# The second mixer's attention: every second head's turned probabilities are copied by ScalarE, and a head's score bank is released by VectorE's first read

## The chip, the cores and the metric

One core of a Trainium2 chip runs the whole kernel. The metric is the device time of one execution in microseconds (us); of several runs the median is taken. TensorE multiplies matrices and writes its results to PSUM, eight banks called bank[0] to bank[7]; VectorE (DVE) and ScalarE (ACT) read them there; GpSimd (POOL) fills a few tiles; SyncE (SP) starts the transfers.

## What is computed

Three transformer layers on 256 tokens of width 1024, all in 32-bit floats. The second layer's mixer is the one of the change. It projects the tokens (`proj = h @ w_in`), cuts the result and runs two attentions of 8 heads of width 64 each:

```python
def mixer_cd(h, w_in, w_out, rel_table):
    ...
    o_c = moba_attention(qc.reshape(B, S, H, dh), kc.reshape(B, S, G, dh), vc.reshape(B, S, G, dh),
                         rel_table[:, :H])
    o_d = stick_breaking_attention(qd.reshape(B, S, H, dh), kd.reshape(B, S, H, dh), vd.reshape(B, S, H, dh))
    return jnp.concatenate([o_c, o_d], axis=-1) @ w_out
```

With 256 tokens the first (moba) is a causal softmax attention with a bias by distance: softmax(scale * q k + bias) v. The second (stick-breaking) has no softmax. With z = scale * q k and a strict causal mask, its weight is

```python
        log_1m = jnp.where(strict, jax.nn.log_sigmoid(-z), 0.0)
        after = lax.cumsum(log_1m, axis=3, reverse=True) - log_1m
        w = jnp.where(strict, jnp.exp(jax.nn.log_sigmoid(z) + after), 0.0)
        o = jnp.einsum('bhqk,bkhd->bqhd', w.astype(dt), v)
```

## The kernel before, in words

Each engine has its own program, written out in order, and they meet only at semaphores: `then_inc(name, 1)` on an instruction counts up when it ends, `wait_ge(name, n)` holds an engine's queue until the count is n. Nothing is scheduled by a planner; the order of the lines is the order on each engine. The weights stream in as units of 128x1024, each split into a high part (ScalarE, L836) and a low part (VectorE, L1403), and each product is done as three matmuls (L2131 to L2133).

The stage of the change lies between the projections of the second mixer (18 units) and its output projection (`cd_out`, 8 units). It is a loop over rounds s = 0 to 9 on TensorE, 0 to 8 on VectorE and ScalarE. One round handles one moba head and one stick-breaking head side by side; scores tiles are 128x384 (the first 128 queries against 128 keys, the second 128 against 256). Moba heads are numbered 24 to 31 in the semaphores.

TensorE in round s, in this order:
- `scores_and_z(s)`, L2690 to L2694: the scores of both heads, moba into bank[4], stick-breaking (z) into bank[5]. It waits until VectorE has read both banks of the round before (neg_ready, and zabs_ready, which L1876 counts).
- `transposes` (L2301) of moba head s-1, 3 of 128x128 into bank[6]. It waits for the probabilities and for `pt_ready`: the copy of the head before out of the same bank[6].
- `stick_suffix(s-1)`, L2703 to L2705: the sums over later keys, into bank[7]. It waits for L1912.
- `pv` (L2311 to L2313): turned probabilities of head s-2 times its values. It waits for their copy (`pt_ready`).
- in odd rounds from 3, `stick_out`, L2715 and L2718: weights times values for a pair of stick-breaking heads. Then the next round's scores. In round 8 the first unit of the output projection (L2131 to L2133) stands behind `pv`, and round 9 has `pv` of the last head.

VectorE in round s:
- `neg_scores` (L1550, L1552): bias added to the moba scores, and the row's minimum; two instructions, each with a small one that reads out the minimum.
- `stick_in(s)`: L1873 adds the mask to z (the first read of bank[5], and the only one), L1876 takes the absolute value from the SBUF copy.
- L1904: suffix sums added to z of head s-1, for the weight.
- `take_pt` (L1560): copies the turned probabilities of moba head s-1 from bank[6] to pt, 128x384. It waits for the transposes and for the `pv` of the head before (pv_done), since both use the same tile pt[:, 0].
- L1912, for head s, after ScalarE's logarithm; then the next round.

ScalarE in round s:
- `exp_rows` (L963): the exponentials of the moba head in two pieces, each with a read-out of its row sum.
- `stick_log`: L1195 (exponential) and L1196 (logarithm).
- L1216: the exponential that gives the weights of stick-breaking head s-1.
- near the end `stick_high` (L971) and the splits (L836) of the output projection's units.

The earlier mixer has a copy of turned probabilities on ScalarE (`ab_take_pt`, L1117); in this stage all 8 are VectorE's L1560.

Of the kernel before, what the change touches and what calls it, by code (L numbers as in the profile page):

```python
# [24 lines left out]
ALU = mybir.AluOpType  # L25
# [15 lines left out]
EPS = 1e-6  # L41
BIG = 1e30
# [139 lines left out]
def build_program(nc, A):  # L182
    with ExitStack() as ctx:
# [85 lines left out]
        rel_landed = sem("rel_landed")  # L269
        cs_ready = sem("cs_ready")  # L270
        raw_full = [sem(f"raw_full{i}") for i in range(RING)]
# [8 lines left out]
        shift_psum = sem("shift_psum")  # L280
        kc_zero = sem("kc_zero")
        cw_landed = sem("cw_landed")
# [13 lines left out]
        sh_ready = sem("sh_ready")  # L296
        warm_ready = sem("warm_ready")
        crow_psum = sem("crow_psum")
# [36 lines left out]
        oTH_ready = sem("oTH_ready")  # L335
        z_psum = sem("z_psum")
        zabs_ready = sem("zabs_ready")
        zlog_ready = sem("zlog_ready")
# [15 lines left out]
        csil_ready = sem("csil_ready")  # L354
        eps_ready = sem("eps_ready")
        dve_done = sem("dve_done")
# [434 lines left out]
        @block.gpsimd  # L791
        def _(pool):
            nc.gpsimd.memset(warm, 1.0).then_inc(warm_ready, 1)
            nc.gpsimd.memset(kc[:, :, :], 0.0).then_inc(kc_zero, 1)
            nc.gpsimd.memset(epst[:, :], EPS).then_inc(eps_ready, 1)

            pool.wait_ge(rstd_ready, 1)
            nc.gpsimd.memset(cs, BIG).then_inc(cs_ready, 1)

            pool.wait_ge(table_out, 16)  # L800
            pool.wait_ge(mod_used, 11)
            pool.wait_ge(shift_psum, 1)
            for half in range(2):
                if half == 1:
                    pool.wait_ge(misc_taken, misc["cscore"] + 1)
                for a in (0, 4, 1, 5, 2, 6, 3, 7):

                    diag = bass.AP(A["table"].tensor, 4 * half * 1024 + 2 * (P - 1 - a),
                                   [[8 * 1024 - 2 * 8, COPIES], [1024, 4], [1, 2 * S]])
                    pool.dma_start(strips[a:P:8, 4 * half:4 * half + 4].rearrange("p a s j -> p a (s j)"),  # L810
                                   diag).then_inc(strips_landed[half], 16)

        @block.scalar
        def _(act):
# [255 lines left out]
            nc.scalar.preload_act_table_set("natural_log_exp_and_others")  # L1070
            act.wait_ge(eps_ready, 1)
            norm_a(0)
# [133 lines left out]
            for h in range(H + 1):  # L1206
                if 1 <= h < H:
                    act.wait_ge(pt_psum, 24 + h)
                    exp_rows(24 + h, 0)
                if 1 <= h < H:  # L1210
                    stick_log(h)
                if h == H:
                    stick_high(2)
                if h >= 1:
                    act.wait_ge(fw_ready, h)
                    nc.scalar.activation(stick_w[(h - 1) % 3], stick_w[(h - 1) % 3], ACT.Exp).then_inc(w_ready, 1)  # L1216
                if h == H - 1:
                    stick_high(0, 2)
# [166 lines left out]
        def _(dve):  # L1385
# [410 lines left out]
            for s in range(AB_STEPS):  # L1796
# [20 lines left out]
                if s == 2:  # L1817
                    take("vrep")
                    rep = bank[7][:, 0:P].rearrange("p (g d) -> p g d", g=G)
                    for t in range(4):  # L1820
                        hm = bcast(const("headmask").rearrange("p (g t) -> p t g", g=G)[:, t].unsqueeze(2), [P, G, HD])
                        V.tensor_tensor(vcb(t).rearrange("p (g d) -> p g d", g=G), rep, hm, ALU.mult)
                    dve.wait_ge(kc_zero, 1)
                    link(V.tensor_copy(kc[0:HD, 0, 0:NCMP], bank[7][0:HD, P:P + NCMP]))
                    taken(V.tensor_copy(kc[HD:P, 1, 0:NCMP], bank[7][HD:P, P:P + NCMP]))
                if s == 3:
                    take("cscore")
                    dve.wait_ge(cs_ready, 1)
                    for q in range(QT):
# [38 lines left out]
            def stick_in(h):  # L1868

                dve.wait_ge(z_psum, h + 1)  # L1870
                if h >= 2:
                    dve.wait_ge(fw_ready, h - 1)
                link(V.tensor_tensor(stick_z_buf[h % 2], bank[5][:, 0:384], mask, ALU.add))  # L1873
                if h >= 2:
                    dve.wait_ge(suf_psum, h - 1)
                V.scalar_tensor_tensor(out=stick_sp[h % 2], in0=stick_z_buf[h % 2], scalar=-1.0,  # L1876
                                       in1=stick_z_buf[h % 2], op0=ALU.mult, op1=ALU.max).then_inc(zabs_ready, 1)
# [14 lines left out]
            for s in range(H + 1):  # L1892
# [3 lines left out]
                if s >= 1:  # L1896
# [5 lines left out]
                    if h >= 3:  # L1902
                        dve.wait_ge(stick_pv, h - 2)
                    V.tensor_tensor(stick_w[h % 3], bank[7][:, 0:384], stick_z_buf[h % 2],  # L1904
                                    ALU.add).then_inc(fw_ready, 1)
                    take_pt(24 + h)
                if s == 1:
# [214 lines left out]
        def _(pe):  # L2122
# [315 lines left out]

            pe.wait_ge(warm_ready, 1)
            def keep_warm(bk, n):  # L2440
# [240 lines left out]
            def scores_and_z(s):  # L2681
# [6 lines left out]
                pe.wait_ge(neg_ready, 24 + s)  # L2688
                pe.wait_ge(zabs_ready, s)
                mm(bank[4][:, P:3 * P], mq[:, P:2 * P], mk, start=True, stop=True, skip_group_check=True)  # L2690
# [311 lines left out]
```

## Time and profile before

| | us |
|---|---|
| median of 3 runs (942.99 to 943.42) | 943.39 |
| the profiled execution, its own time | 944.02 |
| its span, first to last instruction | 942.2 |
| busy: TensorE | 919.1 |
| busy: TensorE's weight loads | 837.8 |
| busy: VectorE | 796.2 |
| busy: ScalarE | 564.9 |
| busy: GpSimd | 8.9 |

All numbers of the trace are from the one profiled execution; its own time is 1.8 us above its span and 0.6 us above the median of the runs. The granted clock of TensorE is the share of its full clock that it was allowed; its mean is 0.999. Matmuls overlap, so the distance from start to start tells more than their durations. A timeline row gives the start in us from the span's start, the duration in us, the engine, the line, the operation, what it writes and reads, how many instructions the row merges (x2), and in brackets the idle time of the engine before it with what ended it.

### The profile page before, as it was taken

To read this page: it belongs to the slowest core of one execution; us is meant where nothing else is said; L and a number is where in the kernel's file an instruction comes from. 1 tells how busy PE (TensorE), PEld (TensorE's weight loads), DVE (VectorE), ACT (ScalarE), POOL (GpSimd) and SP (SyncE) were. 2 spreads that over 40 slices of the span, in tenths; PEclk is the share of its full clock that TensorE was granted. 3 is DMA by queue.
4 is the path that set the end of the run, shared out by engine and by line. 5 is a ranking of instruction groups with operands and counts; after the bars stand their busy time and mean duration, and the time that the engine had idled before them with its cause. 6 is when DMAs were issued, how large, how long until landed. Compare 5 with 4: busy or idle time off the path is not lost. (4 is left out here: it accounts for less than half of the span.)

```text
span 942.2 us, 17752 instructions
## 1 busy us (share of the span) xinstructions
PE 919.1 (98%) x6693; PEld 837.8 (89%) x6693; DVE 796.2 (85%) x1441; ACT 564.9 (60%) x1173; POOL 8.9 (1%) x24
## 2 busy tenths in 40 slices
PE   8999999999999999999999999999999999999997
PEld 5787768999999989977999999998989999999995
DVE  5879897998888879898899988878889778887775
ACT  3447776555444576574745454447857677767774
POOL 0101000000000000000000000000000000000000
PEclk9999999999999999999999999999999999999999
DMA  9996774899988739904499988872832545555531
GB/s 353 397 360 227 263 255 182 317 349 322 342 313 312 257 111 342 345 30 155 166 325 355 315 305 310 312 253 94 333 113 79 200 165 199 190 195 180 180 111 46
DMA packets 63223, 227.46 MB, mean 241 GB/s; under 512 B 7187, under 2 KB 7827, under 8 KB 63158
## 3 DMA queue, kind: packets, MB, share of 16 engines
q1 hardware_dynamic: 62102, 223.86, 66.6%
q0 software_dynamic: 768, 2.10, 0.8%
q8 instruction: 39, 0.64, 0.3%
q10 hardware_dynamic: 288, 0.66, 0.2%
q14 instruction: 26, 0.21, 0.1%
HBM read 225.01 MB, written 1.57 MB: 240 GB/s over the span
## 5 line engine op out<-in xcount | busy, mean ns | idle before, releaser
L2131 PE MATMUL bank<-hH,wH 128*128 128x258 f32 (+1 forms) x1344 | 382.8, 285 | 0.0
L2132 PE MATMUL bank<-hL,wH 128*128 128x258 f32 (+1 forms) x1344 | 379.7, 283 | 0.0
L2133 PE MATMUL bank<-hH,wL 128*128 128x258 f32 (+1 forms) x1344 | 379.2, 282 | 0.0
L1403 DVE TENSOR_TENSOR wL<-raw,wH 128x1024 fp32r<-128x1024 f32 x264 | 320.4, 1219 | 12.7 <-ACT wH L836 10.4
L836 ACT ACTIVATE wH<-raw 128x1024 fp32r<-128x1024 f32 x264 | 269.8, 1047 | 17.3 <-PE bank L2133 14.6
L2131 PEld LDWEIGHTS bank<-hH,wH 128*128 128x128 f32 x1344 | 253.2, 188 | 6.1 <-issue 3.3
L2132 PEld LDWEIGHTS bank<-hL,wH 128*128 128x128 f32 x1344 | 254.6, 189 | 2.3
L2133 PEld LDWEIGHTS bank<-hH,wL 128*128 128x128 f32 x1344 | 254.8, 190 | 0.0
L2131 PE MATMUL bank<-wH,aH 128*128 128x512 f32 x280 | 110.1, 393 | 0.0
L2133 PE MATMUL bank<-wH,aL 128*128 128x512 f32 x280 | 109.1, 390 | 0.0
L2132 PE MATMUL bank<-wL,aH 128*128 128x512 f32 x280 | 109.0, 389 | 0.0
L988 ACT ACTIVATE fcol<-bank 128x1 f32<-128x1 f32 x132 | 14.9, 164 | 112.0 <-PE bank L2133 111.9
L1427 DVE CUSTOM_DVE_ANT_0 modbuf<-modbuf,crow,gw 128x1024 f32<-128x1024 f32 x48 | 62.9, 1317 | 0.0
L2133 PEld LDWEIGHTS bank<-wH,aL 128*128 128x128 f32 x280 | 52.5, 188 | 11.0
L2131 PEld LDWEIGHTS bank<-wH,aH 128*128 128x128 f32 x280 | 52.5, 187 | 10.7 <-issue 2.5
L2132 PEld LDWEIGHTS bank<-wL,aH 128*128 128x128 f32 x280 | 52.6, 188 | 8.3
L1427 DVE CUSTOM_DVE_ANT_0 modbuf<-modbuf,crow,sc 128x1024 f32<-128x1024 f32 x41 | 54.8, 1337 | 0.4 <-DMA modbuf<-in_mods 0.3
L1040 ACT ACTIVATE aH<-sn 128x256 fp32r<-128x256 f32 x66 | 27.6, 418 | 42.8 <-DVE sn L1663 21.5
L1427 DVE CUSTOM_DVE_ANT_0 modbuf<-modbuf,crow,mv 128x1024 f32<-128x1024 f32 x40 | 51.1, 1277 | 1.8 <-DMA modbuf<-in_mods 1.8
L1622 DVE TENSOR_TENSOR sn<-bank,rstd 128x256 f32<-128x256 f32 x44 | 18.6, 422 | 35.9 <-ACT fcol L988 35.9
L1005 ACT ACTIVATE sn<-sn,fcol 128x256 f32<-128x256 f32 x44 | 22.5, 511 | 42.2 <-DVE sn L1622 42.2
L1648 DVE SCALAR_TENSOR_TENSOR pr<-sq,par,pr 128x255 f32<-128x255 f32 x44 | 19.3, 481 | 26.5 <-ACT pr L1020 26.5
(377 smaller groups left out, 1222.0 us busy)
## 6 DMA issues: line engine op xcount, KB each, us to landing
raw<-in_weights SPq DMA_DIRECT2D x264, 512.0 KB, 4.8
modbuf<-in_mods SPq DMA_DIRECT2D x129, 512.0 KB, 6.7
raw<-in_mods SPq DMA_DIRECT2D x10, 512.0 KB, 10.9
strips<-bias_table POOLq DMA_DIRECT2D x16, 128.0 KB, 6.0
strips<-in_mods SPq DMA_DIRECT2D x3, 512.0 KB, 15.0
modbuf<-in_weights SPq DMA_DIRECT2D x3, 512.0 KB, 14.1
x<-in_xT SPq DMA_DIRECT2D x2, 512.0 KB, 4.2
proj<-in_mods SPq DMA_DIRECT2D x2, 512.0 KB, 14.7
```

Source lines behind the costliest of these rows:

```text
L836: nc.scalar.activation(wH[:, slot, :], raw[:, slot, :], ACT.Copy).then_inc(hi_ready[c], 1)
L988: last = nc.scalar.activation(fcol[:, t % 2, n:n + 1], bk[:, S:S + 1], ACT.Copy)
L1005: nc.scalar.activation(sn[:, t % 2, 0:S], sn[:, t % 2, 0:S], ACT.Silu, bias=fcol[:, t % 2, 0:1]).then_inc(silu_ready, 1)
L1040: nc.scalar.activation(aH[:, a_slot(phase, t), :], sn[:, t % 2, S:2 * S], ACT.Copy).then_inc(aH_ready, 1)
L1403: V.tensor_tensor(wL[:, slot, :], raw[:, slot, :], wH[:, slot, :].bitcast(F32), ALU.subtract).then_inc(lo_ready[c], 1)
L1427: V.tensor_tensor_reduce(src, src, crow[:, m // 4, :], weight, total, ALU.mult, ALU.add, total).then_inc(mod_used, 1)
L1622: V.tensor_tensor(sn[:, t % 2, 0:S], gate_bank[:, 0:S], rstd[:, :], ALU.mult).then_inc(g_scaled, 1)
L1648: chain.inc(V.scalar_tensor_tensor(out=dst[:, 1:S], in0=z[:, 0:S - 1], scalar=row[:, 4 * n:4 * n + 1], in1=dst[:, 1:S], op0=ALU.mult, op1= ...
L2131: mm(out, lhs_h, rhs_h, start=start, stop=False, skip_group_check=True)
L2132: mm(out, lhs_h, rhs_l, start=False, stop=False, skip_group_check=True)
L2133: return mm(out, lhs_l, rhs_h, start=False, stop=stop, skip_group_check=True)
```

## The change

ScalarE gets a copy in rounds 2, 4, 6 and 8, behind L1216: the turned probabilities of moba heads 1, 3, 5 and 7 of the stage. VectorE's `take_pt` stays for heads 0, 2, 4 and 6. VectorE's L1873 counts a new semaphore, z_taken, on which both VectorE itself (in the place of a chain semaphore) and TensorE's `scores_and_z` wait; TensorE waited for zabs_ready (L1876) before. Four semaphores of GpSimd's fills at the start become one, pool_set, with counts 1 to 4. The diff:

```diff
--- before.py
+++ after.py
@@ -267,7 +267,6 @@
         con_landed = sem("con_landed")
         x_landed = [sem(f"x_landed{i}") for i in range(2)]
         rel_landed = sem("rel_landed")
-        cs_ready = sem("cs_ready")
         raw_full = [sem(f"raw_full{i}") for i in range(RING)]
         hi_ready = [sem(f"hi_ready{i}") for i in range(3)]
         lo_ready = [sem(f"lo_ready{i}") for i in range(3)]
@@ -278,7 +277,6 @@
         mod_used = sem("mod_used")
         c_landed = sem("c_landed")
         shift_psum = sem("shift_psum")
-        kc_zero = sem("kc_zero")
         cw_landed = sem("cw_landed")
         cwv_landed = sem("cwv_landed")
         table_half = sem("table_half")
@@ -294,7 +292,7 @@
         x_ready = sem("x_ready")
         y_ready = sem("y_ready")
         sh_ready = sem("sh_ready")
-        warm_ready = sem("warm_ready")
+        pool_set = sem("pool_set")
         crow_psum = sem("crow_psum")
         crow_ready = sem("crow_ready")
         unit_full = [sem(f"unit_full{i}") for i in range(6)]
@@ -334,6 +332,7 @@
         oT_ready = sem("oT_ready")
         oTH_ready = sem("oTH_ready")
         z_psum = sem("z_psum")
+        z_taken = sem("z_taken")
         zabs_ready = sem("zabs_ready")
         zlog_ready = sem("zlog_ready")
         sp_ready = sem("sp_ready")
@@ -352,7 +351,6 @@
         zc_ready = sem("zc_ready")
         conv_ready = sem("conv_ready")
         csil_ready = sem("csil_ready")
-        eps_ready = sem("eps_ready")
         dve_done = sem("dve_done")
         act_done = sem("act_done")
         qk_sq = sem("qk_sq")
@@ -790,12 +788,12 @@
 
         @block.gpsimd
         def _(pool):
-            nc.gpsimd.memset(warm, 1.0).then_inc(warm_ready, 1)
-            nc.gpsimd.memset(kc[:, :, :], 0.0).then_inc(kc_zero, 1)
-            nc.gpsimd.memset(epst[:, :], EPS).then_inc(eps_ready, 1)
+            nc.gpsimd.memset(warm, 1.0).then_inc(pool_set, 1)
+            nc.gpsimd.memset(kc[:, :, :], 0.0).then_inc(pool_set, 1)
+            nc.gpsimd.memset(epst[:, :], EPS).then_inc(pool_set, 1)
 
             pool.wait_ge(rstd_ready, 1)
-            nc.gpsimd.memset(cs, BIG).then_inc(cs_ready, 1)
+            nc.gpsimd.memset(cs, BIG).then_inc(pool_set, 1)
 
             pool.wait_ge(table_out, 16)
             pool.wait_ge(mod_used, 11)
@@ -1068,7 +1066,7 @@
                     nc.scalar.preload_act_table_set("natural_log_exp_and_others")
 
             nc.scalar.preload_act_table_set("natural_log_exp_and_others")
-            act.wait_ge(eps_ready, 1)
+            act.wait_ge(pool_set, 3)
             norm_a(0)
             act.wait_ge(par_landed, 16)
             first_row(0)
@@ -1214,6 +1212,10 @@
                 if h >= 1:
                     act.wait_ge(fw_ready, h)
                     nc.scalar.activation(stick_w[(h - 1) % 3], stick_w[(h - 1) % 3], ACT.Exp).then_inc(w_ready, 1)
+                if h >= 2 and h % 2 == 0:
+                    act.wait_ge(pt_psum, 24 + h)
+                    act.wait_ge(pv_done, 24 + h - 1)
+                    nc.scalar.activation(pt[:, 0, 0:384], bank[6][:, 0:384], ACT.Copy).then_inc(pt_ready, 1)
                 if h == H - 1:
                     stick_high(0, 2)
             split_upto(base + 24)
@@ -1820,12 +1822,12 @@
                     for t in range(4):
                         hm = bcast(const("headmask").rearrange("p (g t) -> p t g", g=G)[:, t].unsqueeze(2), [P, G, HD])
                         V.tensor_tensor(vcb(t).rearrange("p (g d) -> p g d", g=G), rep, hm, ALU.mult)
-                    dve.wait_ge(kc_zero, 1)
+                    dve.wait_ge(pool_set, 2)
                     link(V.tensor_copy(kc[0:HD, 0, 0:NCMP], bank[7][0:HD, P:P + NCMP]))
                     taken(V.tensor_copy(kc[HD:P, 1, 0:NCMP], bank[7][HD:P, P:P + NCMP]))
                 if s == 3:
                     take("cscore")
-                    dve.wait_ge(cs_ready, 1)
+                    dve.wait_ge(pool_set, 4)
                     for q in range(QT):
                         n = (7, NCMP)[q]
                         dst = cs[:, q * P:(q + 1) * P].rearrange("p (g t n) -> p g t n", g=G, n=16)[:, :, :, 0:n]
@@ -1870,7 +1872,8 @@
                 dve.wait_ge(z_psum, h + 1)
                 if h >= 2:
                     dve.wait_ge(fw_ready, h - 1)
-                link(V.tensor_tensor(stick_z_buf[h % 2], bank[5][:, 0:384], mask, ALU.add))
+                V.tensor_tensor(stick_z_buf[h % 2], bank[5][:, 0:384], mask, ALU.add).then_inc(z_taken, 1)
+                dve.wait_ge(z_taken, h + 1)
                 if h >= 2:
                     dve.wait_ge(suf_psum, h - 1)
                 V.scalar_tensor_tensor(out=stick_sp[h % 2], in0=stick_z_buf[h % 2], scalar=-1.0,
@@ -1903,7 +1906,8 @@
                         dve.wait_ge(stick_pv, h - 2)
                     V.tensor_tensor(stick_w[h % 3], bank[7][:, 0:384], stick_z_buf[h % 2],
                                     ALU.add).then_inc(fw_ready, 1)
-                    take_pt(24 + h)
+                    if h % 2 == 0:
+                        take_pt(24 + h)
                 if s == 1:
                     values(VALUES["cd"][17])
                 if s < H:
@@ -2436,7 +2440,7 @@
                             mm(out[:, c], row, start_values[:, c, cols], start=False, stop=True,
                                skip_group_check=True).then_inc(unit_used[c], 1)
 
-            pe.wait_ge(warm_ready, 1)
+            pe.wait_ge(pool_set, 1)
             def keep_warm(bk, n):
 
                 for _ in range(n):
@@ -2686,7 +2690,7 @@
                 mq, mk = proj[m_rows, h % 4, :], proj[m_rows, 4, :]
                 zq, zk = proj[z_rows, 5 + s // 2, :], proj[z_rows, 9 + s // 2, :]
                 pe.wait_ge(neg_ready, 24 + s)
-                pe.wait_ge(zabs_ready, s)
+                pe.wait_ge(z_taken, s)
                 mm(bank[4][:, P:3 * P], mq[:, P:2 * P], mk, start=True, stop=True, skip_group_check=True)
                 mm(bank[5][:, 0:S], zk[:, 0:P], zq, start=True, stop=True, skip_group_check=True)
                 mm(bank[4][:, 0:P], mq[:, 0:P], mk[:, 0:P], start=True, stop=True,
```

## Rows read from the trace of the kernel before

**Rows 1.** The page's first line.
```profile
span 942.2 us, 17752 instructions
```

**Rows 2.** Busy by stretch: length, PE, PEld, DVE, ACT, POOL, clock, DMA, GB/s.
```profile
404.82:408.23 3.41, 3.15 (x23) 2.63 (x23) 3.07 (x11) 2.54 (x7) 0.00 (x0) 1.00 0.00 0
...
411.81:415.23 3.42, 3.31 (x26) 2.75 (x26) 3.08 (x9) 2.54 (x7) 0.00 (x0) 1.00 0.00 0
415.23:418.81 3.58, 3.44 (x29) 2.85 (x30) 3.15 (x10) 2.54 (x7) 0.00 (x0) 1.00 0.00 0
```

**Rows 3.** Timeline of VectorE, rounds 2 and 3.
```profile
406.90 0.55 DVE L1560 COPY pt<-bank 128x384 f32<-128x384 f32 x1
407.75 0.56 DVE L1912 SCALAR_TENSOR_TENSOR otok<-sq,otok 128x384 f32<-128x384 f32 x1 [0.31 <-ACT otok L1196]
408.23 0.28 DVE L1550 CUSTOM_DVE_ANT_0 sn<-bank,strips 128x128 f32<-128x128 f32 x1
...
409.85 0.55 DVE L1904 TENSOR_TENSOR pt<-bank,sq 128x384 f32<-128x384 f32 x1
410.31 0.55 DVE L1560 COPY pt<-bank 128x384 f32<-128x384 f32 x1
411.16 0.56 DVE L1912 SCALAR_TENSOR_TENSOR otok<-sq,otok 128x384 f32<-128x384 f32 x1 [0.30 <-ACT otok L1196]
411.81 0.29 DVE L1550 CUSTOM_DVE_ANT_0 sn<-bank,strips 128x128 f32<-128x128 f32 x1
```

**Rows 4.** Timeline of ScalarE, the same rounds.
```profile
407.63 0.51 ACT L1216 ACTIVATE sn<-sn 128x384 f32<-128x384 f32 x1
408.96 0.40 ACT L963 ACTIVATE pr<-sn,nm 128x128 f32<-128x128 f32 x1 [0.82 <-DVE nm L1552]
...
410.52 0.62 ACT L1196 ACTIVATE otok<-otok,con 128x384 f32<-128x384 f32 x1
411.04 0.51 ACT L1216 ACTIVATE pt<-pt 128x384 f32<-128x384 f32 x1
```

**Rows 5.** Timeline of TensorE, rounds 2 to 4.
```profile
403.25 0.45 PE L2690 MATMUL bank<-proj 64*128 64x256 f32 x1 [0.66 <-DVE otok L1876]
...
407.59 0.52 PE L2301 MATMUL bank<-con,pr 128*128 128x128 f32 x3
408.37 0.49 PE L2703 MATMUL bank<-otok,con 128*128 128x128 f32 x2 [0.26 <-DVE otok L1912]
...
409.35 0.33 PE L2311 MATMUL bank<-vt,pt 128*128 128x64 f32 x2
...
410.06 0.43 PE L2715 MATMUL bank<-pr,vt 128*64 128x256 f32 x1
...
410.86 0.48 PE L2690 MATMUL bank<-proj 64*128 64x256 f32 x1
...
411.71 0.55 PE L2301 MATMUL bank<-con,pr 128*128 128x128 f32 x3
412.10 0.39 PE L2703 MATMUL bank<-otok,con 128*128 128x128 f32 x2
...
412.97 0.34 PE L2311 MATMUL bank<-vt,pt 128*128 128x64 f32 x2
```

**Rows 6.** The earlier mixer's copy on ScalarE: durations in ns, min/median/max.
```profile
L1117 ACT ACTIVATE pt<-bank x24: 463/476/492, 68.3 to 135.6; 128x384 f32<-128x384 f32 x24
```

**Rows 7.** Timeline of all engines, the stage's end.
```profile
426.76 0.33 PE L2311 MATMUL bank<-vt,pt 128*128 128x64 f32 x2
...
427.55 0.52 ACT L1216 ACTIVATE sn<-sn 128x384 f32<-128x384 f32 x1 [1.25 <-DVE sn L1904]
427.65 0.56 DVE L1560 COPY pt<-bank 128x384 f32<-128x384 f32 x1
427.98 1.04 ACT L836 ACTIVATE wH<-raw 128x1024 fp32r<-128x1024 f32 x1
...
430.23 0.33 PE L2311 MATMUL bank<-vt,pt 128*128 128x64 f32 x2
```

## The prediction

> **What bounds the kernel now.** I read the page first: the span is 942.2 us [rows 1] and TensorE is at work nearly all of it, so anything that makes TensorE wait and is not caught up later is paid in full. Then I cut the stage of the change, the attention of the second mixer, into its rounds. A round of the loop over heads handles one head; its mark is VectorE's bias-and-minimum (L1550). The stretches are cut at these marks: round 2 from 404.82, round 3 from 408.23, round 4 from 411.81, round 5 from 415.23, round 6 from 418.81. An even round takes 3.41 or 3.42 us, an odd one 3.58, so a pair costs 7.00 us; in round 2 TensorE is busy for 3.15 us and the granted clock is 1.00, its upper level of 2.4 GHz [rows 2]. Then I followed one pair on each engine in time order.
>
> VectorE [rows 3]: from mark to mark it has no hole but one, before L1912, 0.31 us in one round and 0.30 us in the next, and it ends on ScalarE's L1196. In the round that starts at 408.23 it also waits before the next mark: L1912 to L1550 is 0.48 us when free (407.75 to 408.23) and 0.65 us there (411.16 to 411.81), the difference of 0.17 us being TensorE's scores.
>
> ScalarE [rows 4]: the exponentials (L963) start 0.73 us after the mark (408.23 to 408.96), the logarithm's second half (L1196) 1.56 us after that, L1216 0.52 us later, and then nothing until the next L963: 0.82 us of idle time in the round from 408.23. L1912 starts 0.64 us after L1196. So the loop is VectorE's mark, ScalarE's exponentials and logarithm, VectorE's L1912, mark: 0.73 + 1.56 + 0.64 + 0.48 = 3.41 us, which is the round. VectorE's copy of the turned probabilities (L1560) is beside this loop, under ScalarE's logarithm.
>
> TensorE [rows 5]: transposes (L2301), suffix sums (L2703), the product with the values (L2311), every second round the product of the stick-breaking heads (L2715), then the next scores (L2690). The transposes of head 2 start at 407.59, which is 0.14 us after the end of VectorE's copy of head 1 (406.90 + 0.55 = 407.45 [rows 3]): they go into the one bank that this copy empties. This hand-over is what the change moves.
>
> **The change part by part.** *The copy of heads 1, 3, 5 and 7 leaves VectorE.* Four times L1560, each some 0.46 us of VectorE's issue (L1904 at 409.85 to L1560 at 410.31 [rows 3]). VectorE then only waits longer for L1196 before L1912: 0.30 us becomes about 0.76 us. Gain on the path: none; the cover is ScalarE's chain from L963 to L1196. If that cover were gone, it would be worth up to 4 x 0.46 = 1.84 us.
>
> *The same copy on ScalarE, behind L1216.* The earlier mixer already has this instruction, 128x384 from a bank on ScalarE: 0.476 us in the median, 0.463 to 0.492 [rows 6]. What follows L1216 starts about 0.43 us after it (427.55 to 427.98 [rows 7]). In ScalarE's own queue it costs nothing: 0.91 us fall into the hole before L963, behind L1216 at 407.63 it would run 408.06 to 408.54, and L963 is due at 408.96. That leaves 0.42 us. The two waits ahead of it (transposes of the head, values product of the head before) are over by then.
>
> The copy is later, though: 408.06 instead of 406.90. Its waiter is TensorE. Taking 0.13 us to TensorE (0.14 from VectorE; I take nearly the same), the transposes of head 2 start at 408.67 instead of 407.59, 1.08 us late. Behind them in the queue stand the suffix sums, the values product, the stick-breaking product and the scores of round 4. From here with the free spacings of [rows 5]: transposes to suffix 0.39 (411.71 to 412.10), suffix to values product 0.87 (412.10 to 412.97), then 0.71 and 0.80, so suffix 409.06, product 409.93, L2715 410.64, scores 411.44 against 410.86. The hold-ups of before (TensorE waited 0.26 us at L2703) absorb half of the 1.08 us. The scores reach VectorE 0.95 us after their start (410.86 to 411.81), so the mark of round 4 comes at 412.39 against 411.81: **+0.58 us**.
>
> The loop of two rounds is now another one, through ScalarE's copy and TensorE's queue: mark to L963 0.73, L1196 1.56, L1216 0.52, copy 0.43, its length 0.48, to TensorE 0.13, suffix 0.39, product 0.87, L2715 0.71, scores 0.80, next even mark 0.95. Sum 7.57 us against 7.00: **+0.57 us**, once, from round 4 to round 6. That makes 1.15 us at the mark of round 6, 419.96.
>
> *The third hand-over* has no scores behind it. From 419.96 the transposes of head 6 start 3.85 us later, at 423.81; suffix 424.20, product 425.07, L2715 425.78, transposes of head 7 426.58, suffix of head 7 not before 426.97. The other gate is VectorE: the mark of round 7 at 419.96 + 3.41 = 423.37, L1912 by ScalarE at 423.37 + 2.93 = 426.30, but the copy that VectorE keeps (head 6) waits for the end of the values product, 0.89 us after that product's start (426.76 to 427.65 [rows 7]), so 425.96, and with 0.46 us L1912 comes at 426.42. In the round of 407.75 L2703 starts 0.62 us after L1912 [rows 3, 5], so suffix 7 starts at 427.04 and, with the 0.98 us that a held suffix takes before the values product (408.37 to 409.35 [rows 5]), that product starts at 428.02 against 426.76 [rows 7]: +1.26 us. Earlier, in rounds 3 and 5, the same small delay of L1912 (0.1 us) is hidden, since VectorE waits for the scores anyway. Sum **+1.2 to 1.3 us**; I take 1.2.
>
> *The fourth* costs nothing: behind suffix 7 TensorE goes to the output projection, and the values product of head 7 stands at 430.23, 2.7 us after L1216 at 427.55 [rows 7], where copy and way need 1.04 us. If that projection were not there it would cost some 0.5 us.
>
> *Head's bank freed by the first read.* TensorE waits for z_taken (L1873) instead of zabs_ready (L1876), some 0.6 us earlier. Only the row at 403.25 shows TensorE idle for it, 0.66 us [rows 5]. Its scores are for the mark at 404.82, which they would meet at 403.25 + 0.95 = 404.20 already, and the transposes behind them wait for VectorE's copy as before. Worth nothing now; at most 0.17 us at each of two marks if the hand-over before them were not late. The wait on VectorE itself replaces a wait of the same kind.
>
> *Semaphores merged for GpSimd's fills.* Same instructions in the same order, each waiter asks for the count of its own fill: nothing, with a bound of 0.1 us either way.
>
> **A page against the rows.** The Trainium skill, "TensorEngine Tiling (Array Packing)", PSUM Bottleneck, advises to use ScalarE as well as VectorE to empty PSUM; it would make this change a gain, and it is my second rival below. "PSUM — Partial Sum Buffer", Engine vs sequencer instructions, calls ScalarE's queue strictly first in, first out; by that the copy cannot slip ahead of L1216 into an earlier place, and the rows of ScalarE agree, being in program order. Without these two sentences the sum stands as it is.
>
> **Forecast.** 1.2 us later than the kernel before. Against the profiled execution, whose span is 942.2 us and whose own time is 944.02 us, that is a span of 943.4 and a time of 945.2 us. Against the median of the runs, 943.39 us (0.6 lower than the profiled one), it is **944.6 us**. About 0.2%, 1.9 us here, is what a measurement of this kernel can tell from no change; the forecast lies inside it, on the slow side. Chance 0.70.
>
> **Rivals.** *Slower, beyond 0.2%: the lateness isn't absorbed.* Place: TensorE's queue behind L2301 in rounds 3, 5 and 7. The price is the whole 1.08 us each time, 3 x 1.08 = 3.2 us, 946.6 us. It decides if TensorE's stretch between the copy and the next even mark grows by as much play as it now has, 0.5 us: L1912 of the odd rounds has only 0.1 us of play against VectorE's remaining copy, and a late L1912 holds the suffix sums. Against it: each free spacing is a row of the trace. A lower granted clock in the longer holes of TensorE would act likewise, but the rows show 1.00 across the present ones. Chance 0.13.
>
> *Faster: VectorE's issue is the bound.* Its row is 3.07 us busy of 3.41 [rows 2]. If L1912 really followed VectorE's own queue, the four copies would give back 1.84 us and the earlier bank 2 x 0.17: 941.2 us. This is what the tiling page would have. Against it: L1912 idles for ScalarE in both rounds. Chance 0.04.
>
> *Nothing: the copy's move is hidden and so is the rest.* It needs TensorE to have 1.08 us of play between L2301 and the even mark; it has about 0.5. Or the delay is made up later, in the projection, where TensorE rarely waits. 943.4 us, at best 0.34 less for the marks' waits: 943.1. Chance 0.13.
>
> **Numbers.** The range leaves out the fast rival and most of the slow one: 943.2 to 946.0. It holds the bounds of the way to TensorE (0.05 to 0.25 us, three times) and of L1912's play. Faster by over 0.2%: 0.03. Within: 0.80, which is the "nothing" case and nearly all of the forecast. Slower: 0.17, the slow rival and the upper edge of the forecast.
>
> **What the next profile would show.** Right: four ScalarE copies of 0.48 us right behind L1216 in the even rounds; L2301 of rounds 3, 5, 7 released by ScalarE with about 1 us of idle TensorE ahead; pairs of rounds at 7.57 us; VectorE idle near 0.76 us before L1912 in even rounds, and before the even marks 0.6 us or more for TensorE; suffix 7 near 427.0. Wrong: even marks on their old places, a copy that starts earlier than L1216, or pairs of 8 us.

## The result, and the profile after

The changed kernel takes 944.85 us in the median of 20 runs (943.65 to 946.13), the kernel before 943.43 us (942.50 to 945.93, 20 runs beside them). The ratio is 1.0013, 95% interval 1.0007 to 1.0019: 1.2 us slower, 0.7 to 1.8 us (the two medians differ by 1.4 us). That is inside the 0.2% that was called no change, and on the slow side, as forecast (944.6 us). The spans of the two profiled executions can't show it alone: 942.7 us against 942.2 [rows 1]. The stage itself can, since there are hardly any transfers in it and its distances repeat from pair to pair.

The lines of the changed kernel are shifted: the mark of a round is L1552 (was L1550), VectorE's copy L1562 (L1560), its others L1879 (L1876), L1907 (L1904) and L1916 (L1912); on ScalarE L961, L1193, L1194, L1214 (L963, L1195, L1196, L1216) and the new copy L1218; on TensorE L2305 (L2301), L2707 (L2703), L2315 (L2311), L2719 (L2715), L2694 and L2696 (L2690 and L2692). The experiments shift them by a few lines more; the operation and its tiles tell which is meant.

Busy time of the changed kernel by stretch, from mark to mark, rounds 2 to 5 (columns as in [rows 2]):

```profile
404.06:407.48 3.42, 2.61 (x20) 2.26 (x20) 2.62 (x10) 2.64 (x8) 0.00 (x0) 1.00 0.00 0
407.48:411.60 4.12, 3.70 (x32) 3.13 (x33) 3.29 (x11) 2.70 (x8) 0.00 (x0) 1.00 0.02 4
411.60:415.02 3.42, 2.79 (x23) 2.44 (x23) 2.62 (x9) 2.63 (x8) 0.00 (x0) 1.00 0.00 0
415.02:419.14 4.12, 3.70 (x32) 3.13 (x33) 3.29 (x10) 2.71 (x8) 0.00 (x0) 1.00 0.00 0
```

Even rounds are as long as before, odd ones 4.12 us instead of 3.58 [rows 2]: a pair costs 7.54 us instead of 7.00. VectorE did lose its work, 2.62 us busy in round 2 instead of 3.07, and got nothing for it. The granted clock stays at 1.00.

ScalarE in rounds 2 and 3 of the changed kernel:

```profile
406.87 0.51 ACT L1214 ACTIVATE sn<-sn 128x384 f32<-128x384 f32 x1
407.29 0.47 ACT L1218 ACTIVATE pt<-bank 128x384 f32<-128x384 f32 x1
408.46 0.40 ACT L961 ACTIVATE pr<-sn,nm 128x128 f32<-128x128 f32 x1 [0.70 <-PE bank L2305]
...
409.35 0.51 ACT L1193 ACTIVATE otok<-otok 128x384 f32<-128x384 f32 x1
```

TensorE:

```profile
401.90 0.45 PE L2694 MATMUL bank<-proj 64*128 64x256 f32 x1
...
403.43 0.52 PE L2305 MATMUL bank<-con,pr 128*128 128x128 f32 x3 [0.60 <-DVE pt L1562]
...
407.90 0.52 PE L2305 MATMUL bank<-con,pr 128*128 128x128 f32 x3 [1.08 <-ACT pt L1218]
408.25 0.39 PE L2707 MATMUL bank<-otok,con 128*128 128x128 f32 x2
...
409.13 0.33 PE L2315 MATMUL bank<-vt,pt 128*128 128x64 f32 x2
...
410.64 0.48 PE L2694 MATMUL bank<-proj 64*128 64x256 f32 x1
```

VectorE, from the end of round 2 to the mark of round 4:

```profile
407.00 0.56 DVE L1916 SCALAR_TENSOR_TENSOR otok<-sq,otok 128x384 f32<-128x384 f32 x1 [0.77 <-ACT otok L1194]
407.48 0.28 DVE L1552 CUSTOM_DVE_ANT_0 sn<-bank,strips 128x128 f32<-128x128 f32 x1
...
410.02 0.56 DVE L1562 COPY pt<-bank 128x384 f32<-128x384 f32 x1
410.54 0.56 DVE L1916 SCALAR_TENSOR_TENSOR otok<-sq,otok 128x384 f32<-128x384 f32 x1
411.60 0.29 DVE L1552 CUSTOM_DVE_ANT_0 sn<-bank,strips 128x128 f32<-128x128 f32 x1 [0.51 <-PE bank L2696]
```

Read in this order, the rows show the path of the delay. The copy runs 407.29 to 407.76. TensorE, idle for 1.08 us, starts the transposes at 407.90, 3.84 us after the mark of round 2 (404.06); before it was 2.77 us (404.82 to 407.59 [rows 3, 5]). Three pieces of TensorE's work later the scores of round 4 start at 410.64, and VectorE, idle for 0.51 us, gets them at 411.60.

For the experiments one measure serves: **the stretch** from TensorE's first scores of the loop to its values product of head 6, the last one ahead of the output projection. Before it is 26.89 us (399.87 to 426.76), after 28.10 us (399.12 to 427.22): +1.21 us. The 0.75 us by which the loop itself starts earlier in the second profile lie ahead of every copy that was moved. The start lies at 398.92 to 399.87 in the fourteen profiles of this study, and at 398.92, 399.13, 399.29, 399.32, 399.37 and 399.87 in the six whose program ahead of the loop is that of the kernel before. What is lost in the stretch isn't made up later: from its end to the end of the span there are 515.4 to 515.6 us in all fourteen.

### The profile page after: what moved, and what is told of

Same layout as the page of the kernel before. It is cut to its first block and busy times, and to the rows that moved or that the text cites. A ratio compares the mean times of both kernels' runs of the same rounds, so it can differ in the third digit from the quotient of the medians.

```text
span 942.7 us, 17752 instructions
## 1 busy us (share of the span) xinstructions
PE 917.7 (97%) x6693; PEld 837.5 (89%) x6693; DVE 794.9 (84%) x1437; ACT 566.2 (60%) x1177; POOL 8.9 (1%) x24
## 5 line engine op out<-in xcount | busy, mean ns | idle before, releaser
L1038 ACT ACTIVATE aH<-sn 128x256 fp32r<-128x256 f32 x66 | 27.6, 417 | 42.6 <-DVE sn L1665 21.5
L1650 DVE SCALAR_TENSOR_TENSOR pr<-sq,par,pr 128x255 f32<-128x255 f32 x44 | 19.3, 481 | 26.8 <-ACT pr L1018 26.8
```

Source lines behind the costliest of these rows:

```text
L1038: nc.scalar.activation(aH[:, a_slot(phase, t), :], sn[:, t % 2, S:2 * S], ACT.Copy).then_inc(aH_ready, 1)
L1650: chain.inc(V.scalar_tensor_tensor(out=dst[:, 1:S], in0=z[:, 0:S - 1], scalar=row[:, 4 * n:4 * n + 1], in1=dst[:, 1:S], op0=ALU.mult, op1= ...
```

## The experiments

Theory A is that of the forecast: what costs is the late hand-over of bank[6] to TensorE, through what stands behind it in TensorE's queue. Theory B: ScalarE's additional copy costs as such. Theory C: the release of bank[5] by z_taken matters. Where the text gives "one time", the kernel ran once; such a time can't tell differences of this size, and the stretch is read there.

### Each half of the change alone

Both start from the changed kernel. The copies alone:

```diff
-                pe.wait_ge(z_taken, s)
+                pe.wait_ge(zabs_ready, s)
```

> The change without its second half: ScalarE copies heads 1, 3, 5 and 7, but TensorE's scores wait for zabs_ready (the second read's count) as before. Measure: TensorE from its first scores of the loop to the values product of head 6 (30 in the semaphores' numbering): 26.89 us in the kernel before, 28.10 in the changed one. Theory A (the late hand-over of bank[6] costs, nothing else): 28.0 to 28.2 us, time 1.2 us over the kernel before. Theory C (the earlier release of bank[5] costs or saves something): the stretch departs from 28.10 by over 0.2 us.

The release alone:

```diff
-                if h >= 2 and h % 2 == 0:
-                    act.wait_ge(pt_psum, 24 + h)
-                    act.wait_ge(pv_done, 24 + h - 1)
-                    nc.scalar.activation(pt[:, 0, 0:384], bank[6][:, 0:384], ACT.Copy).then_inc(pt_ready, 1)
...
-                    if h % 2 == 0:
-                        take_pt(24 + h)
+                    take_pt(24 + h)
```

> The change without its first half: VectorE copies all eight heads, TensorE's scores wait for z_taken, and GpSimd's fills share one semaphore. Theory A: the stretch is 26.8 to 26.95 us as before, the scores of round 2 start 0.6 us earlier and that shortens nothing; time within 0.2 us of the kernel before. Theory C: over 0.3 us away from 26.89.

The copies alone: stretch 28.10 us (399.49 to 427.59), 944.91 us, ratio 1.0013 (1.0004 to 1.0022). The release alone: stretch 26.90 us (399.17 to 426.07), 943.75 us, ratio 1.0002 (0.9993 to 1.0011). In the stretch the first half is the whole effect and the second is nothing, though it does what it says; the times agree, with intervals of 0.8 to 0.9 us either way. TensorE's transposes and scores around round 2, first with the copies alone, then with the release alone:

```profile
402.87 0.45 PE L2694 MATMUL bank<-proj 64*128 64x256 f32 x1 [0.67 <-DVE otok L1879]
...
403.81 0.52 PE L2305 MATMUL bank<-con,pr 128*128 128x128 f32 x3
```

```profile
401.96 0.45 PE L2689 MATMUL bank<-proj 64*128 64x256 f32 x1
...
403.48 0.52 PE L2300 MATMUL bank<-con,pr 128*128 128x128 f32 x3 [0.60 <-DVE pt L1558]
```

With the release alone the wait for the second read (0.67 us) is gone, and 0.60 us of TensorE's idle time stand before the next group instead, the transposes, which wait for VectorE's copy.

### The same copies at another place

The changed kernel, with ScalarE's copy moved up by one instruction (e3):

```diff
                 if 1 <= h < H:
                     stick_log(h)
...
+                if h >= 2 and h % 2 == 0:
+                    act.wait_ge(pt_psum, 24 + h)
+                    act.wait_ge(pv_done, 24 + h - 1)
+                    nc.scalar.activation(pt[:, 0, 0:384], bank[6][:, 0:384], ACT.Copy).then_inc(pt_ready, 1)
                 if h >= 1:
                     act.wait_ge(fw_ready, h)
                     nc.scalar.activation(stick_w[(h - 1) % 3], stick_w[(h - 1) % 3], ACT.Exp).then_inc(w_ready, 1)
-                if h >= 2 and h % 2 == 0:
-                    act.wait_ge(pt_psum, 24 + h)
-                    act.wait_ge(pv_done, 24 + h - 1)
-                    nc.scalar.activation(pt[:, 0, 0:384], bank[6][:, 0:384], ACT.Copy).then_inc(pt_ready, 1)
```

> The changed kernel with ScalarE's copy one instruction earlier, ahead of the exponential of the weights instead of behind it: same work on ScalarE, the copy ends 0.4 to 0.5 us sooner. Theory A: lateness at the transposes of heads 2, 4 and 6 falls from 1.08 to about 0.6 us, of which 0.5 is absorbed; pairs of rounds at 7.05 to 7.15 us instead of 7.54, the stretch at 27.0 to 27.3 us, time 0.1 to 0.4 over the kernel before. Theory B (it is ScalarE's extra work or the copy out of PSUM beside VectorE that costs, wherever it stands): the stretch stays at 28.0 or more.

The changed kernel, with the even heads on ScalarE and the odd ones on VectorE (e4):

```diff
-                if h >= 2 and h % 2 == 0:
+                if h % 2 == 1:
                     act.wait_ge(pt_psum, 24 + h)
-                    act.wait_ge(pv_done, 24 + h - 1)
+                    if h >= 2:
+                        act.wait_ge(pv_done, 24 + h - 1)
...
-                    if h % 2 == 0:
+                    if h % 2 == 1:
                         take_pt(24 + h)
```

> The same number of copies on ScalarE, but of heads 0, 2, 4 and 6, behind the exponential of the weights in the odd rounds; VectorE copies 1, 3, 5 and 7. The late hand-over now stands before the transposes of the even rounds, which have no product of the stick-breaking heads behind them and whose scores come 0.6 us before VectorE wants them. Theory A: the lateness is absorbed, the stretch is 26.9 to 27.3 us, time 0 to 0.4 us over the kernel before. Theory B: as in the changed kernel, 28 us or more.

The copy ahead of the weights' exponential: stretch 27.15 us (399.48 to 426.63), 943.92 us, ratio 1.0003 (0.9994 to 1.0012). The marks of rounds 4 and 6, 7.13 us apart:

```profile
411.55 0.29 DVE L1552 CUSTOM_DVE_ANT_0 sn<-bank,strips 128x128 f32<-128x128 f32 x1 [0.22 <-PE bank L2696]
...
418.68 0.29 DVE L1552 CUSTOM_DVE_ANT_0 sn<-bank,strips 128x128 f32<-128x128 f32 x1 [0.22 <-PE bank L2696]
```

The same four copies, 0.42 us sooner, and 0.95 of the 1.21 us are gone: the work of the copies as such (theory B) isn't what costs. The 0.26 us left lie in rounds 3 and 5, 3.72 and 3.71 us long instead of 3.58, at whose ends VectorE waits for the scores as the rows show.

The even heads: stretch 27.60 us (399.37 to 426.97), 944.45 us, ratio 1.0010 (0.9999 to 1.0020). Within the loop it came as expected: the marks of rounds 4 and 6 lie at 411.48 and 418.48, 7.00 us apart as before, with ScalarE making a copy in each odd round. The 0.71 us, where 0 to 0.4 were expected, come at its two ends: 0.13 in round 2 (3.54 us long), 0.54 in round 8. TensorE's transposes, rounds 2, 4 and 8:

```profile
404.78 0.52 PE L2306 MATMUL bank<-con,pr 128*128 128x128 f32 x3 [1.66 <-ACT pt L1219]
...
411.74 0.52 PE L2306 MATMUL bank<-con,pr 128*128 128x128 f32 x3 [0.29 <-ACT pt L1219]
...
425.73 0.52 PE L2306 MATMUL bank<-con,pr 128*128 128x128 f32 x3 [1.14 <-ACT pt L1219]
```

In round 4 the wait of 0.29 us is absorbed: no stick-breaking product follows, and the next scores have time. In round 8 the transposes start 3.83 us after the mark of round 7 (421.90) instead of 2.78, 1.05 us late. Half of that is taken up on the way to the values product, which starts 5.07 us after that mark instead of 4.53; no mark of VectorE follows that could take up the rest, and behind it comes the projection. I had left out the end of the loop when I wrote down 27.3 us.

### What the lateness runs into

TensorE's scores ahead of the stick-breaking product, on the kernel before (e6) and on the changed one (e7):

```diff
+            scores_and_z(1)
             for s in range(H + 2):
-                if 1 <= s < H:
-                    scores_and_z(s)
                 if 1 <= s <= H:
...
+                if 1 <= s < H - 1:
+                    scores_and_z(s + 1)
                 if s >= 3 and s % 2 == 1:
                     stick_out((s - 3) // 2)
```

> The kernel before with TensorE's scores of the next round ahead of the product of the stick-breaking heads in rounds 3 and 5. Theory A: VectorE no longer waits 0.17 us before the marks of rounds 4 and 6; all rounds 3.41 us, the stretch 26.5 to 26.6 us instead of 26.89. Nothing a time can show.

> The changed kernel with the same move on TensorE: scores of the next round ahead of the product of the stick-breaking heads. Theory A: ScalarE's copy is as late as in the changed kernel and TensorE still waits about 1.0 us for it at the transposes of heads 2, 4 and 6, but the way from there to the even marks is 0.80 us shorter, so that the loop through the copy is 6.77 us and no longer bounds: pairs at 6.9 to 7.0 us, the stretch 26.7 to 27.1 us, time within 0.3 us of the kernel before. Theory B (the wait of TensorE itself is what costs, wherever the scores stand): 28 us.

On the kernel before: all rounds 3.41 us, the stretch 26.58 us (399.13 to 425.71), as expected, with one time of 943.02 us. On the changed kernel: 27.38 us (399.09 to 426.47), 944.09 us, ratio 1.0009 (1.0000 to 1.0018). TensorE still waits for the copy:

```profile
407.92 0.52 PE L2305 MATMUL bank<-con,pr 128*128 128x128 f32 x3 [1.08 <-ACT pt L1218]
...
415.08 0.52 PE L2305 MATMUL bank<-con,pr 128*128 128x128 f32 x3 [0.67 <-ACT pt L1218]
```

The stretch is 0.72 us shorter than in the changed kernel, but 0.31 of that is what this order also gives without the offload (26.89 to 26.58). Like with like, the offload costs 0.80 us in this order (27.38 against 26.58) instead of 1.21: the shorter way to the marks takes away 0.41 us, a third. And 27.38 is over the 27.1 expected. ScalarE in round 4 of this run shows what I had overlooked:

```profile
410.43 0.51 ACT L1214 ACTIVATE pt<-pt 128x384 f32<-128x384 f32 x1
412.10 0.40 ACT L961 ACTIVATE pr<-sn,nm 128x128 f32<-128x128 f32 x1 [1.17 <-PE bank L2305]
```

The mark of round 4 is at 411.03, and the exponentials start 1.07 us after it instead of 0.73: there is one tile for the probabilities of all heads, so they wait until TensorE has turned those of the head before. Late transposes thus hold ScalarE too, and the rounds become 3.54 us (odd) and 3.62 us (even) instead of 3.41. In the changed kernel the same gate is in its rows above (L961 at 408.46, 0.98 us after the mark), without effect there, since round 3 then waits for the scores anyway.

Both repairs together (e9) are the edits of e3 and e7 on the changed kernel.

> The changed kernel with both repairs: ScalarE's copy ahead of the exponential of the weights, and TensorE's scores of the next round ahead of the product of the stick-breaking heads. What e7_change_scores_first left was a second gate: ScalarE's exponentials wait for the transposes of the head before (one tile of probabilities), at 412.10, 0.34 us later than the mark alone would allow. With the copy 0.4 us earlier that gate should be met. Theory A: rounds at 3.41 to 3.46 us, the stretch 26.5 to 26.8 us, that is the kernel before with its waits for the scores removed and no gain from the four copies that VectorE no longer makes. If VectorE's issue did count, it would be under 26.2 us.

Stretch 26.56 us (399.37 to 425.93), one time of 943.20 us. All marks are 3.41 us apart:

```profile
404.33 0.28 DVE L1552 CUSTOM_DVE_ANT_0 sn<-bank,strips 128x128 f32<-128x128 f32 x1
...
407.74 0.28 DVE L1552 CUSTOM_DVE_ANT_0 sn<-bank,strips 128x128 f32<-128x128 f32 x1
...
411.16 0.28 DVE L1552 CUSTOM_DVE_ANT_0 sn<-bank,strips 128x128 f32<-128x128 f32 x1
...
414.57 0.28 DVE L1552 CUSTOM_DVE_ANT_0 sn<-bank,strips 128x128 f32<-128x128 f32 x1
```

With the copies on ScalarE and no harm from their lateness the stretch is what e6 has with all copies on VectorE, 26.56 against 26.58 us. That is the value of VectorE's four saved copies in this order: nothing.

### What bounds the round of 3.41 us

Another order inside the round, on the kernel before (e5), first on ScalarE, then on VectorE:

```diff
                 if 1 <= h < H:
-                    act.wait_ge(pt_psum, 24 + h)
-                    exp_rows(24 + h, 0)
+                    stick_log(h)
                 if 1 <= h < H:
-                    stick_log(h)
+                    act.wait_ge(pt_psum, 24 + h)
+                    exp_rows(24 + h, 0)
...
-                    neg_scores(24 + s, MOBA_ORDER[s])
                     stick_in(s)
+                    neg_scores(24 + s, MOBA_ORDER[s])
```

The kernels e8 and e12 are the edits of e5 and e6 together, e10 those of e5 and e7, and e11 is e8 with `stick_suffix(s - 1)` ahead of `transposes(24 + s - 1, 3)` on TensorE.

> The kernel before with another order inside a round: VectorE reads the stick-breaking scores (mask, absolute value) ahead of the moba head's minimum, and ScalarE does the exponential and logarithm of the stick-breaking head ahead of the moba exponentials. Theory A says that the loop of 3.41 us goes through the absolute value, ScalarE's logarithm and L1912, not through VectorE's busy time: without the minimum and the moba exponentials ahead of them it is about 0.59 + 0.59 + 0.56 + 0.64 + 0.48 = 2.86 us, so VectorE's own 3.07 us or TensorE's rounds (mean 3.2 us) bound it, and the stretch falls from 26.89 to 25.0 to 25.8 us, the time by 1.1 to 1.9 us. Theory B (VectorE's and ScalarE's issue bounds the round whatever the order): 26.6 us or more.

> Both orders on the kernel before: stick-breaking head first on VectorE and ScalarE, scores first on TensorE. Theory A: as e5_stick_first or up to 0.5 us shorter, stretch 24.6 to 25.6 us, time 1.2 to 2.2 us under the kernel before, which would beat both kernels. Theory B: 26.5 us or more.

The new order alone: stretch 26.55 us, above the 25.0 to 25.8 expected, with one time of 943.26 us. It did shorten the even rounds (marks at 405.32 and 408.34, 3.02 us, in which VectorE is never idle), so with all eight copies on VectorE a round can be shorter than 3.41 us: the amount of VectorE's work wasn't its bound. But the odd ones became 4.03 us. Within the loop TensorE and VectorE now wait mainly here:

```profile
PE bank L2301 <- ACT pr L963: 2.3, 5, 0.6
PE bank L2690 <- DVE nm L1552: 0.6, 1, 0.6
```

```profile
DVE sq L1873 <- PE bank L2694: 1.2, 2, 0.6
```

VectorE waits twice 0.6 us for the scores behind the stick-breaking product. With the scores first (e8) that wait goes, and the stretch is 25.98 us (399.29 to 425.27), the time 942.63 us, ratio 0.9993 (0.9984 to 1.0003). That missed too: 24.6 to 25.6 us and 1.2 to 2.2 us under the kernel before were expected.

> e8_both_orders once more, the same file, for its interval: the stretch 25.98 us, 0.9 us under the kernel before in the trace, and a time 0.5 to 1.3 us under it (a ratio of 0.9986 to 0.9995).

The same kernel again: stretch 26.04 us, 942.35 us, ratio 0.9991 (0.9982 to 1.0000). TensorE's three waits for the moba exponentials are left, 1.6 us in all:

```profile
PE bank L2301 <- ACT pr L963: 1.6, 3, 0.6
PE bank L2690 <- DVE nm L1552: 0.6, 1, 0.6
```

> The changed kernel with the order of e8_both_orders: stick-breaking head first on VectorE and ScalarE, scores first on TensorE. ScalarE's copy now stands behind logarithm, moba exponentials and weights, 3.08 us after the mark of the even round, where in e8_both_orders the transposes start 2.22 us after it. TensorE has almost no play there. Theory A: the loop through the copy is about 7.06 us against 6.57 in e8_both_orders, the stretch 26.8 to 27.6 us against 25.98: the offload costs more, not less, in the faster order. Theory B (VectorE is the bound of the faster order, so the offload pays): under 25.8 us.

The changed kernel's copies in this order: stretch 27.65 us (399.28 to 426.93), just over the 26.8 to 27.6 expected, one time of 944.27 us. The transposes of round 3:

```profile
408.31 0.52 PE L2305 MATMUL bank<-con,pr 128*128 128x128 f32 x3 [1.33 <-ACT pt L1218]
```

The marks of rounds 4 and 6 lie 7.22 us apart (7.06 expected: VectorE reaches that mark 0.1 us after its scores allow, held by its own copy, which waits for the late values product). Against e8 the offload now costs 1.67 us: in the order in which the mean round of VectorE is nearest to its busy time, taking work off it costs most. TensorE has less play for the late hand-over: the transposes of round 3 are 0.87 us later after the mark of round 2 than in e8 (3.09 us against 2.22) and the mark of round 4 0.84 us later (7.21 against 6.37), where the order of the kernel before took up half. This order with the copy earlier in ScalarE's queue was not run, so whether the offload could pay in it stays open.

> e8_both_orders with TensorE's suffix sums ahead of the transposes. In e8_both_orders TensorE waits three times, 1.6 us in all, for the moba exponentials at the transposes, while L1912, which frees the suffix sums, is done 0.1 to 0.3 us earlier. The stretch 25.6 to 25.95 us instead of 25.98; time 0.9 to 1.5 us under the kernel before. If the exponentials behind the later transposes come late: 26.0 to 26.5 us.

This one missed: 26.80 us (398.92 to 425.72), 0.8 us longer, 943.44 us, ratio 0.9994 (0.9985 to 1.0003). Its waits:

```profile
PE bank L2703 <- DVE otok L1912: 2.6, 6, 0.8
DVE pt L1560 <- PE bank L2313: 1.9, 7, 0.5
```

VectorE's copy waits for the values product of the head before, which shares its tile pt[:, 0]. With the transposes between the suffix sums and that product, the product comes later, VectorE's copy with it, and L1912 behind the copy in VectorE's queue, for which the suffix sums wait. From start to start that is L1912 to suffix sums 0.60 (406.65 to 407.25), to transposes 0.99, to values product 0.32, to copy 0.89, to L1912 0.47: 3.27 us, which is the length of this run's shorter rounds. A loop that I had not drawn.

## Why the prediction was right

The size came out, and so did the path on which it is lost: 1.2 us forecast, 1.2 us in the ratio (0.7 to 1.8), 1.21 us in the stretch. After the mark of round 2 the delay is 0.55 us at the mark of round 4, 1.09 at the mark of round 6 and 1.22 at the values product of head 6, where 0.58, 1.15 and 1.26 were forecast. But two gates were named wrongly or not at all, without harm to the sum; they stand at their places below.

- *The copy leaves VectorE, gain none.* Right. Idle before L1916 in round 2 went from 0.31 to 0.77 us (0.76 forecast). e9 against e6 shows the value of the four copies as 0.02 us. But the loop of 3.41 us was drawn through the wrong member. The prediction leads it from the mark over ScalarE's exponentials (0.73) to L1196 (1.56). Rows of the changed kernel, rounds 2 and 3, show what the instruction ahead of L1194, the exponential L1193, starts on:

```profile
404.80 0.40 ACT L961 ACTIVATE pr<-sn,nm 128x128 f32<-128x128 f32 x1 [0.83 <-DVE nm L1554]
...
405.20 0.56 DVE L1879 SCALAR_TENSOR_TENSOR otok<-sq 128x384 f32<-128x384 f32 x1
...
405.80 0.52 ACT L1193 ACTIVATE otok<-otok 128x384 f32<-128x384 f32 x1
...
408.61 0.56 DVE L1879 SCALAR_TENSOR_TENSOR otok<-sq 128x384 f32<-128x384 f32 x1
```

In round 2 it starts 1.00 us after L961 and 0.04 us after the end of VectorE's absolute value (L1879, 405.76). In round 3, where L961 is late (408.46) and the absolute value has ended at 409.17, it starts 0.89 us after L961 (409.35). So the exponentials have 0.1 us to spare in a free round, and the loop goes through VectorE's minimum, mask and absolute value, then the logarithm and L1912, as the expectation of e5 has it. The sum stays 3.41 us, since both ways end at L1193. In this order moving the copy gains nothing either way, because it stands behind the absolute value on VectorE.
- *The copy on ScalarE costs nothing in its own queue.* Right: 0.47 us, 0.42 us behind L1214 (0.476 and 0.43 forecast), and it ends 0.70 us ahead of the next exponentials.
- *Late hand-over at the transposes.* Right: 3.84 us after the mark of the even round against 3.85 forecast, and 0.14 us from ScalarE's end to TensorE where I took 0.13.
- *The loop of two rounds, 7.57 us.* Measured 7.54 (411.60 to 419.14). e3, which shortens one link of it by 0.42 us, shortens the pair by 0.41 (7.13).
- *Third hand-over, +1.26 us in all at the values product of head 6.* From the mark of round 2 that product is at 23.16 us in the changed kernel (404.06 to 427.22) and was at 21.94 before (404.82 to 426.76): +1.22. Here the number owes something to luck. The prediction takes VectorE's remaining copy (head 6) as the gate of L1912. The rows of round 7:

```profile
424.97 0.62 ACT L1194 ACTIVATE otok<-otok,con 128x384 f32<-128x384 f32 x1
...
425.11 0.56 DVE L1562 COPY pt<-bank 128x384 f32<-128x384 f32 x1
...
425.62 0.56 DVE L1916 SCALAR_TENSOR_TENSOR otok<-sq,otok 128x384 f32<-128x384 f32 x1
...
426.24 0.49 PE L2707 MATMUL bank<-otok,con 128*128 128x128 f32 x2
...
427.22 0.33 PE L2315 MATMUL bank<-vt,pt 128*128 128x64 f32 x2
```

The copy alone would let L1916 start at 425.57 to 425.59 (0.46 to 0.48 us behind it, as in e8 and e10, where nothing else holds it); the logarithm lets it start 0.65 us behind L1194, at 425.62. The logarithm ends last, by 0.03 to 0.05 us, because the exponentials ahead of it waited for the late transposes. The prediction had put ScalarE's way 0.12 us ahead of the copy's; both ways came out nearly the same, so the term held.
- *L1912 of odd rounds 0.1 us late, hidden.* Right in effect: 3.06 us after the mark (407.48 to 410.54) instead of 2.93. Not in cause: the copy at 410.02 would have allowed 410.48 to 410.50, and again the logarithm is last, since the exponentials wait for the late transposes, a gate that the prediction didn't name. The changed kernel pays nothing for it there; e7 does.
- *Fourth hand-over free.* Right: with the odd heads, the last copy lies behind the projection's first unit. The even heads in e4 show the price if it doesn't: 0.54 us, near the 0.5 that the prediction puts on one that isn't hidden.
- *The bank's earlier release, nothing.* Right (e2), and the idle time moved one instruction on, as written.
- *Merged semaphores, nothing.* Not tried by itself, and not shown to 0.1 us. Outside the stretch the profiled spans are 914.4 to 915.3 us in the six kernels with separate semaphores and 914.6 to 915.0 in the eight with the one.

Of the rivals, "not absorbed" (3.2 us) was wrong because the lateness did meet play, about half of it. "Nothing" was wrong because there was only that half, and none is made up later (515.4 to 515.6 us behind the stretch in every profile). "VectorE's issue is the bound" is refuted for this order by e9. The Trainium skill, "TensorEngine Tiling (Array Packing)", PSUM Bottleneck, advises to share the emptying of PSUM between ScalarE and VectorE, for a kernel in which the emptying has become the bottleneck. Here it gave no gain: the stretches with it are 28.10, 27.15 and 27.60 us against 26.89 in the order of the kernel before, 27.38 and 26.56 against 26.58 with the scores first, and 27.65 against 25.98 in the order of e8. ScalarE's queue is strictly first in, first out by the Trainium skill, "PSUM — Partial Sum Buffer", Engine vs sequencer instructions. The trace agrees: the copy starts 0.42 us after L1214 starts, its place in the program, and 0.42 us sooner after the mark when e3 moves it ahead.

One version is faster than the changed kernel, e8: its ratios to the kernel before are 0.9993 and 0.9991 (intervals up to 1.0003 and 1.0000), the changed kernel's is 1.0013 (from 1.0007). Against the kernel before, the trace shows 0.85 to 0.91 us less stage: likely faster, too small to be settled by these runs. It has none of the change in it.

## What to carry to other kernels

A copy taken off a busy engine is worth only what that engine's queue holds up: look for the idle row before the next instruction that others wait for, and if it ends on another engine, as in this stage, the offload is worth nothing. Then ask when the moved instruction will run in its new queue and who waits for it; the price is that lateness, less the play on the way, plus every other tile that the late step keeps occupied. Write the new loop as a sum of start-to-start distances, from mark to mark, and mind the ends of the loop apart, since the play there is another.

## What was not expected of the hardware

Little. A copy of 128x384 out of PSUM takes ScalarE 0.47 us and VectorE 0.55 to 0.56 us in the same loop of the changed kernel. And 0.1 us of what I had read as ScalarE's own time between L961 and L1193 was its wait for VectorE: 0.89 us in round 3 (408.46 to 409.35), 1.00 us in round 2 (404.80 to 405.80).
